# Hybrid decoder step with 64 experts: three of the shared expert's five output tiles moved into the steps 16, 24 and 32 of the expert loop, and the experts' table first filled for four experts

## The reference

```
scores = sigmoid(x @ w_router); top 8 of 64 experts per token (within 4 of 8 groups)
gates  = scores of the chosen / their sum * 2.5
routed = sum over a token's 8 experts of gate * (silu(x @ w1_e) * (x @ w3_e)) @ w2_e
y      = (silu(x @ w1_s) * (x @ w3_s)) @ w2_s  +  routed          # shared expert + routed experts
out    = LayerNorm(ALPHA * x + y)
```

## Time and profile before

| what | value |
|---|---|
| median of three runs | 1242.86 us (1241.7 to 1245.32) |
| the profiled execution: its time | 1241.34 us |
| its span in the trace | 1239.5 us |
| busy PE, DVE, ACT, POOL | 1145.6, 411.7, 257.2, 175.6 us |
| chain that ended last: PE, DMA, DVE | 68%, 15%, 14% of the span |
| HBM read and written | 300.15 and 29.36 MB |

### The profile page before, as it was taken

One profiled execution on the slowest core, in us unless ns is written; L12 is line 12 of the kernel. 1 busy time (PEld: TensorE's weight loads), 2 busy tenths in 40 slices (PEclk: granted clock), 3 DMA queues, 4 the chain that ended last, 5 costly groups with the idle time before them and its releaser, 6 DMA issues.

```text
span 1239.5 us, 21052 instructions
## 1 busy us (share of the span) xinstructions
PE 1145.6 (92%) x8302; PEld 763.2 (62%) x8302; DVE 411.7 (33%) x1016; ACT 257.2 (21%) x564; POOL 175.6 (14%) x208
## 2 busy tenths in 40 slices
PE   7999997999987999889999899998999989989965
PEld 6888645877865688567656565555555556555411
DVE  0359997122067325711221111111211212111124
ACT  1101324022051315011222222221212212212200
POOL 3120040000000000202122122122221222211100
PEclk9999998999999999899999999999999999999977
DMA  9530304034048352619999999999999999999496
GB/s 330 226 136 1 153 12 170 1 135 153 1 141 322 132 216 91 241 51 337 358 378 375 369 376 379 368 376 358 370 370 359 373 378 358 376 359 363 182 357 268
DMA packets 66313, 319.16 MB, mean 257 GB/s; under 512 B 10473, under 2 KB 16833, under 8 KB 39629
## 3 DMA queue, kind: packets, MB, share of 16 engines
q1 hardware_dynamic: 51269, 278.60, 59.5%
q0 software_dynamic: 13568, 35.48, 8.4%
q10 hardware_dynamic: 1424, 4.35, 0.9%
HBM read 300.15 MB, written 29.36 MB: 266 GB/s over the span
## 4 chain that ended last, share of the span: by engine, by line
PE 68%; DMA 15%; DVE 14%; SPq 1%; issue 1%; ACT 1%; DVEq 0%; POOLq 0%
PE psum L744 62%; DMA arena<-in_w_e_dram 10%; DVE act_mem L1698 7%; PE psum L759 6%; DMA arena<-y_rows 3%; DVE mk_mem L1857 2%; DMA arena<-in_w_in_dram 1%; SPq L539 0%; DVE act_mem L1795 0%; DVE act_mem L1712 0%; DVE rstd L1786 0%; DVE act_mem L1793 0%; DVE act_mem L1763 0%; SPq L494 0%; SPq L493 0%
## 5 line engine op out<-in xcount | busy, mean ns | idle before, releaser
L744 PE MATMUL psum<-arena,act_mem 128*32 128x128 f32 (+6 forms) x4800 | 517.0, 365 | 20.8 <-DMA arena<-in_w_e_dram 16.5
L744 PEld LDWEIGHTS psum<-arena,act_mem 128*32 128x32 f32 (+5 forms) x4800 | 266.3, 125 | 210.7 <-issue 118.6
L744 PE MATMUL psum<-act_mem,arena 128*128 128x260 f32 (+1 forms) x1728 | 352.7, 366 | 9.2 <-DMA arena<-in_w_o_dram 3.8
L744 PEld LDWEIGHTS psum<-act_mem,arena 128*128 128x128 f32 x1728 | 306.2, 192 | 53.0 <-DMA arena<-in_w_o_dram 4.7
L759 PE MATMUL psum<-ident,act_mem 96*128 96x96 f32 (+8 forms) x484 | 77.7, 291 | 19.1 <-POOL ident L557 6.8
L667 POOL DMA_INDIRECT y_rows<-act_mem,idx_y x40 | 45.2, 1130 | 323.1 <-DVE idx_x L2074 173.0
L2086 DVE TENSOR_SCALAR act_mem<-psum,act_mem 96x512 f32<-96x512 f32 (+1 forms) x40 | 29.9, 748 | 156.0 <-PE psum L744 156.0
L1698 DVE SCALAR_TENSOR_TENSOR act_mem<-act_mem,wcb 128x511 f32<-128x511 f32 (+29 forms) x120 | 77.7, 725 | 0.0
L759 PEld LDWEIGHTS psum<-ident,act_mem 96*128 96x128 f32 (+8 forms) x484 | 57.5, 175 | 32.3 <-issue 8.0
L2083 DVE TENSOR_TENSOR act_mem<-act_mem,psum 128x192 f32<-128x192 f32 x35 | 12.4, 354 | 191.9 <-ACT act_mem L1554 191.9
L744 PEld LDWEIGHTS psum<-act_mem 128*96 128x96 bf16 (+4 forms) x371 | 28.6, 126 | 57.4 <-issue 51.4
(11 more groups left out here) (262 smaller groups left out, 698.0 us busy)
## 6 DMA issues: line engine op xcount, KB each, us to landing
arena<-in_w_e_dram SPq DMA_DIRECT2D x192, 1024.0 KB
arena<-y_rows SPq DMA_DIRECT2D x8, 2048.0 KB, 23.7
arena<-in_w_in_dram SPq DMA_DIRECT2D x16, 512.0 KB, 18.7
arena<-in_cache_mem_k_dram SPq DMA_DIRECT2D x8, 1024.0 KB, 8.5
arena<-in_cache_mem_v_dram SPq DMA_DIRECT2D x8, 1024.0 KB, 11.4
arena<-in_w_v_dram SPq DMA_DIRECT2D x1, 4096.0 KB, 24.3
arena<-in_w_k_dram SPq DMA_DIRECT2D x1, 4096.0 KB, 13.8
arena<-in_w_out_dram SPq DMA_DIRECT2D x1, 4096.0 KB, 13.8
```

The lines of the kernel that those rows point to most:

```text
L744: return pe.matmul(out, lhsT, rhs, start=first, stop=last)
```

## The change

- `LATE_SO` assigns the tiles 2, 3 and 4 of the shared expert to the steps 16, 24 and 32. In such a step PE runs `shared_out(t)` between `t_step(e-1)` and `c_step(e)`, after waits for the bank of the step before and for a second copy of the weights, `w2s_late` (the place of the first is overwritten in the loop). DVE runs `shared_sum(t)` ahead of its `c_step(e)`; `y_step(e-1)` waits for it.
- Tile 1 is computed between `a_step(1)` and `a_step(2)` as before; tile 0 still comes first. `PAIR` gives them other banks, and the waits that guard the banks move along: `c_step(0)` for tile 0, `y_step(0)` for tile 1, `b_step(0)` for `count`.
- DVE fills the table first for the four experts sorted first (`FIRST`), makes `place` in one operation instead of two (the slot numbers now start at 1), and goes on to the one-hot matrices. `count` and `over` follow after the second one-hot matrix; the table's other 60 experts after `shared_sum(0)`, and `s_table` with them. PE no longer waits for `s_table`.
- SP loads `w2s_late` where it loaded the rows of the last LayerNorm; these are now loaded behind the last expert.
- On PE and DVE the steps 1 to 32 are written out (`UNROLLED`), not 1 to 8.

```diff
+EARLY_SO = 2
+LATE_SO = {t: 2 * NB + NB * (t - EARLY_SO) for t in range(EARLY_SO, TT)}
+PAIR = {f"so{t}": 2 if t == 0 else 0 for t in range(TT)}
+UNROLLED = max(LATE_SO.values()) // NB
+FIRST = 4
...
@@ SP
             wait_out(sp, "count")
-            sp.dma_start(ln3g, ...)
-            sp.dma_start(ln3b, ...)
+            sp.dma_start(w2s_late, I["w2_s"][0].rearrange("(k p) n -> p k n", p=P)).then_inc(s_w2late, 16)
             with sp.Fori(0, E // 4 - 1) as i:
...
+            wait_full(sp, f"so{TT - 1}")
+            sp.dma_start(ln3g, ...)
+            sp.dma_start(ln3b, ...)
...
@@ PE, y_step
+                if isinstance(e, int) and e == 0:
+                    wait_out(pe, "so1")
+                for t, turn_no in LATE_SO.items():
+                    if isinstance(e, int) and e == turn_no - 1:
+                        wait_out(pe, f"so{t}")
...
@@ PE, before the loop
-            shared_out(0)
-            pe.wait_ge(s_table, 1)
-            wait_out(pe, "count")
-            wait_out(pe, "x24")
+            wait_out(pe, "order")
+            shared_out(0, w2s)
...
+            wait_out(pe, "x24")
             a_step(0, 0)
             a_step(1, 1)
-            shared_out(1)
+            wait_out(pe, "rank")
+            shared_out(1, w2s)
             a_step(2, 2)
-            shared_out(2)
             a_step(3, 3)
-            shared_out(3)
-            shared_out(4)
-            wait_out(pe, "so4")
+            wait_out(pe, "count")
             b_step(0, 0, 16)
+            wait_out(pe, "so0")
             c_step(0, 0, 48)
...
@@ PE, step
+                for t, turn_no in LATE_SO.items():
+                    if isinstance(e, int) and e == turn_no:
+                        pe.wait_ge(m_ya, e - 1)
+                        pe.wait_ge(m_yv, len(HEAVY) * i + heavies(k - 2))
+                        pe.wait_ge(s_w2late, 16)
+                        shared_out(t, w2s_late)
                 c_step(e, k % NB, 48 * (2 * i + (k // 4 + 1)))
...
@@ DVE
+            def shares(at):
+                sh, tab = share_p[:, :, at], table[:, :, at]
+                link(dve.tensor_copy(tab[:, :, :, 3], sh))
+                link(dve.tensor_tensor(sh, sh, tab[:, :, :, 3], ALU.subtract))
+                link(dve.tensor_copy(tab[:, :, :, 4], sh))
+                link(dve.tensor_tensor(tab[:, :, :, 5], sh, tab[:, :, :, 4], ALU.subtract))
+            def turns(last, at):
+                for t in range(TT):
+                    n = chain(dve.tensor_tensor_scan(left[:, t, 0:last], wsum[:, 0:last], sel_p[:, t, 0:last], ...))
+                dve.wait_ge(s_v, n)
+                link(dve.tensor_scalar(table[:, :, at, 2], left[:, :, at], 1.0, None, ALU.subtract))
+            shares(slice(0, FIRST))
+            turns(FIRST, slice(0, FIRST))
...
             oh_step(1, 1)
+            wait_full(dve, "count")
...
             shared_sum(0)
-            shared_sum(1)
+            shares(slice(FIRST, E))
+            turns(E, slice(FIRST, E))
+            dve.sem_inc(s_table, 1)
             i_step(2, 2, None)
```

More of the change, by code:

```diff
@@ L78 @@
 TOK = P // TOPK
-PAIR = {f"so{t}": (t + 2) % 3 for t in range(TT)}
+EARLY_SO = 2
[3 more added lines that the diff above has]
+FIRST = 4
 A0, A1, A2, A3, A4 = 0, 4160, 8320, 12480, 16640
@@ L285, in decoder_step @@
         w2s = act_mem[:, 9280:9280 + 2048].rearrange("p (k n) -> p k n", k=2)
+        w2s_late = kv_mem[:, 0:2048].rearrange("p (k n) -> p k n", k=2)
         s_full = sem("s_full")
@@ L1286, in _ @@
             LAST = E // NB - 1
-            for k in range(1, NB + 1):
-                step(k, k, 0)
-            with pe.Fori(1, LAST) as i:
+            for i in range(UNROLLED):
+                for k in range(1, NB + 1):
+                    step(NB * i + k, k, i)
+            with pe.Fori(UNROLLED, LAST) as i:
                 for k in range(1, NB + 1):
@@ L2019, in _ @@
             dve.sem_inc(s_order, 1)
-            link(dve.tensor_copy(table[:, :, :, 3], share_p))
-            link(dve.tensor_tensor(share_p, share_p, table[:, :, :, 3], ALU.subtract))
-            link(dve.tensor_copy(table[:, :, :, 4], share_p))
-            link(dve.tensor_tensor(table[:, :, :, 5], share_p, table[:, :, :, 4], ALU.subtract))
-            for t in range(TT):
-                n = chain(dve.tensor_tensor_scan(left[:, t, :], wsum, sel_p[:, t, :], 0.0, ALU.mult, ALU.add))
-            dve.wait_ge(s_v, n)
@@ L2028, in _ @@
-            link(dve.tensor_scalar(table[:, :, :, 2], left, 1.0, None, ALU.subtract))
-            wait_full(dve, "rank")
-            link(dve.scalar_tensor_tensor(place[:, :, 0:E], bank("rank")[:, 0:TT * E].rearrange("p (t e) -> p t e", t=TT),
-                                          1.0, sel_p, ALU.add, ALU.mult))
-            dve.tensor_scalar(place[:, :, 0:E], place[:, :, 0:E], 1.0, None, ALU.subtract).then_inc(s_emV, 1)
-            wait_full(dve, "count")
-            link(dve.tensor_tensor(mk_mem[:, 520:584], bank("count")[:, 0:E], bump, ALU.add))
@@ new lines, in turns @@
+            def turns(last, at):
+                for t in range(TT):
+                    n = chain(dve.tensor_tensor_scan(left[:, t, 0:last], wsum[:, 0:last], sel_p[:, t, 0:last], 0.0,
+                                                     ALU.mult, ALU.add))
+                dve.wait_ge(s_v, n)
+                link(dve.tensor_scalar(table[:, :, at, 2], left[:, :, at], 1.0, None, ALU.subtract))
+            shares(slice(0, FIRST))
+            turns(FIRST, slice(0, FIRST))
+            wait_full(dve, "rank")
@@ L2039, in _ @@
+            dve.scalar_tensor_tensor(place[:, :, 0:E], bank("rank")[:, 0:TT * E].rearrange("p (t e) -> p t e", t=TT),
+                                     1.0, sel_p, ALU.add, ALU.mult).then_inc(s_emV, 1)
             wait_out(dve, "rank")
-            dve.sem_inc(s_table, 1)
             def shared_sum(t):
@@ L2121, in _ @@
             oh_step(1, 1)
+            wait_full(dve, "count")
+            link(dve.tensor_tensor(counts, bank("count")[:, 0:E], bump, ALU.add))
+            dve.tensor_reduce(cmax, counts, AX.X, ALU.max).then_inc(s_emV, 1)
+            wait_out(dve, "count")
+            dve.tensor_copy(over[:, :], cmax).then_inc(s_over, 1)
             i_step(0, 0, None)
@@ L2126, in _ @@
             shared_sum(0)
-            shared_sum(1)
+            shares(slice(FIRST, E))
+            turns(E, slice(FIRST, E))
+            dve.sem_inc(s_table, 1)
             i_step(2, 2, None)
             oh_step(4, 4)
-            shared_sum(2)
             i_step(3, 3, None)
             oh_step(5, 5)
-            shared_sum(3)
-            shared_sum(4)
+            shared_sum(1)
             c_step(0, 0)
             def step(e, k, i, sc, si):
+                for t, turn_no in LATE_SO.items():
+                    if isinstance(e, int) and e == turn_no:
+                        shared_sum(t)
                 c_step(e, k % NB)
@@ L2145, in _ @@
             LAST = E // NB - 1
-            for k in range(1, NB + 1):
-                step(k, k, 0, None if k <= 2 else 16 * ((k - 1) // 2), None if k < 5 else 16 * ((k - 5) // 2 + 1))
-            with dve.Fori(1, LAST) as i:
+            for i in range(UNROLLED):
+                for k in range(1, NB + 1):
+                    e = NB * i + k
+                    step(e, k, i, None if e <= 2 else 16 * ((e - 1) // 2), None if e < 5 else 16 * ((e - 5) // 2 + 1))
+            with dve.Fori(UNROLLED, LAST) as i:
                 for k in range(1, NB + 1):
```

25 lines of the change are left out of this document (9 added, 16 removed).

## The result

The changed kernel took 1247.51 us (median; 1237.28 to 1253.95 in 20 runs), the kernel before 1242.17 in as many runs beside it: a ratio of 1.0033, 95% interval 1.0019 to 1.0048. It is slower by a third of a per cent; forecast were 1229.0 us (1223 to 1237) and a gain. The profiled execution spans 1247.4 us, against 1239.5 before; its time, 1249.18 us, is 1.7 above the median.

A forecast was written before the change was run, and what follows sets the result against it. Expert loads set the pace from 600 us on, their stream starting a fixed time after the first `c_step`. Gain 14.7 - 1.7 (clock) - 0.7 (written-out steps) = 12.3 us against 1241.34: 1229.0 us, range 1223 to 1237.

The forecast's parts named there:

- Written-out steps: 24 more steps fetched as instructions on PE: 0.25 MB at 370 GB/s, a cost of 0.7 us.
- instruction fetch makes it slower: Rival: 16 fetches in written-out steps stop PE, 1.6 us each, 25.6 us less 12.3 gained: 1254.6 us; chance 0.04.
- The front: Up to the first expert's `b_step(0)` and `c_step(0)`: 14.7 us earlier, less 1.7 for the slow clock.
- the table: DVE's shortened table ahead of the first one-hot matrix: 2.0 us, at 0.25 per small operation and 0.75 for five scans.
- The gather: Gather 0 ahead of `b_step(0)`: issued at 513.0, landing 7.2 us later, with bounds of 3.7 and 11.3 us.
- PE's clock: After 4.3 us of PE idling before `b_step(0)`, the clock halves: 1.7 us charged to `b_step(0)` and `c_step(0)`, at most 3.
- Tiles 2 to 4: Shared-expert tiles in steps 16, 24 and 32: hidden where PE waits for weights, 0 us; uncovered, 3 x 4.2 = 12.6.
- What DVE and POOL now do later: The other 60 experts' table and gathers 2 and 3, after the front: costs nothing; uncovered, 6 us at `b_step(2)`.
- Loads: `w2s_late` replaces LayerNorm rows of as many bytes, now loaded behind expert 63: 0 us, at most 1.
- waits of a microsecond and more without a releaser in the steps 9 to 32: Sign in PE's waits of the changed profile that would show the forecast wrong.
- The DMA share did not fall in the rounds with a tile: Sign in the loop: a fall of the DMA share in rounds with a tile would show the forecast wrong.
- PE did not wait at `b_step(2)`: Sign at the third expert's transposes: a PE wait there would show the forecast wrong.

The follow-up runs named there:

- e9: The kernel before with four rounds written out instead of one, its loop moved by 110 idle TensorE increments placed in waits: 1248.07 us, 1.0037 of before.
- e12: The kernel before with four rounds written out instead of one, its loop moved by 90 idle TensorE increments placed in waits: 1246.48 us, 1.0031 of before.
- e5: The changed kernel with its loop moved by 110 idle TensorE increments placed where PE waits anyway: 1240.12 us, 0.9974 of the kernel before.
- e8: The kernel before with four rounds written out on TensorE and VectorE instead of one, nothing else changed: 1257.6 us, 1.0114 of before.
- e6: The changed kernel with all 64 steps written out and the load of expert 2 held until gather 0 landed: 1232.4 us, 0.9922 of the kernel before.
- e10: e6 with the three tiles at steps 12, 20 and 28 in place of 16, 24 and 32: 1232.39 us, 0.9916 of the kernel before.
- e4: e1 with the loads of experts 2 and 3 issued only when gather 0 has landed: 1240.06 us, 0.9976 of the kernel before.
- e2: The kernel before with 57 idle increments at TensorE's start, moving its loop to the changed kernel's place in a block: 1269.81 us, 1.0218 of before.
- e1: The changed kernel with 110 idle increments at the start of TensorE's stream, moving its loop: 1248.99 us, 1.0053 of the kernel before.
- e11: The changed kernel with gather 0 ahead of experts 2 and 3's loads, tiles at steps 4, 6, 8, one round written out: 1238.95 us, 0.9958 of before.

## Why the prediction was wrong

**The step that failed is "Written-out steps", at 0.7 us.** Measured are 15.1 us from expert 4 to expert 63. I priced a fetch by its bytes, 24 steps at 370 GB/s, and took from one stretch that its latency is hidden. Two things were wrong in this.

First, the 24 written-out steps by themselves cost 4 to 5 us (e9, e12; e5 loses 5.0 between experts 4 and 63). The stretch from 640 to 720 showed no fetch on the chain although the loop was fetched there for the first time: it is no written-out code, as step 9, the first of the loop, began its product at 628. PE waited there for weights too (2.75 us at step 16) and 0.93 us without a releaser at 686; four rounds in a row, with tiles in three of the waits for weights, had less to hide in. That the fetches are what costs the 4 to 5 us is argued, not shown.

Second, and twice as dear: the change moved the loop. Nothing in the prediction asked whether the loop, which cost no fetch before, would still stay in the buffer at its new place. It did not: 10 us (15.1 less 5.0, after against e5), 9.5 by time between e8 and e9, 7.4 between the changed kernel and e5. (The first figure compares two single executions; the profiled one of e5 lies 2.7 us below its median and that of the changed kernel 1.7 above.) Each of the changed kernel's jumps back stalls 4.1 or 5.4 us, and PE comes out of it with the clock down. The rows that could have raised the question were in the profile: no instruction fetch from 720 to 1100 in a program that is 37 packets long.

The Trainium skill, "Runtime: NRT & Kernel Launch" (Instruction fetch mechanics), says that TensorE's buffer holds 2048 instructions and is refilled in blocks of 256, that its refill runs ahead in order, and that a taken branch to a block outside the current window of two blocks stalls for a fetch. The trace agrees with the stall (4.11 and 5.36 us), and the seven or eight blocks fit the size. It differs on the window: the kernel before jumps back over more than six blocks without a fetch. The page also says that the cost of crossing a block is mostly hidden; e9's 18 more packets go with 4 to 5 us.

The rival "instruction fetch makes it slower" named the mechanism with a chance of 0.04. Its price was 1.6 us for each of 16 fetches, 25.6 us, and 0.8 us was where it would have turned the gain. The runs show 18 more packets and 4 to 5 us for the straight steps, some 0.25 us each, and 18 more for the two jumps back. The rival counted the straight steps and not the loop: with those alone (e5) the kernel is faster than before, so its direction came out by luck, through the loop, which it did not name.

**The front was mis-sized: 13.0 us forecast, 8.5 measured** (7.1 at the load of expert 4, plus the 1.4 by which this execution's prefix was late). The chain of waits after, which answers to the earlier trace rows:

```profile
508.40 1.37 DVE act_mem L2035
...
514.03 0.15 DVE idx_x L2076
...
515.06 9.94 DMA act_mem<-x_rows,idx_x
...
525.14 1.73 PE psum L768 x8
...
527.93 9.86 PE psum L753 x64
```

Order and places are as forecast; three terms are off, by 0.7, 2.7 and 0.9 us, nearly all of the 4.5. The cast of 128x20 took 1.37 us, not 0.25, and the table 2.84 (508.40 to 511.24) instead of 2.0, which puts the gather 0.7 behind its forecast. The kernel before could have told: its first cast took 1.87 us and the next one, of the same shape, 0.70, some 1.2 less, as in the changed kernel (1.37 and 0.21). In both, the first cast overlaps POOL's clearing of two buffers, and in the changed one it ends with it. That the clearing is the cause, no run tells. The rows before (two) and after:

```profile
506.50 1.85 POOL L645 MEMSET act_mem<- 128x1024 f32 x2
...
509.57 0.70 DVE L2023 CAST act_mem<-kv_mem 128x320 bf16<-128x320 f32 x1
```

```profile
507.86 1.85 POOL L654 MEMSET act_mem<- 128x1024 f32 x2
```

The gather landed 9.9 us after its issue, not 7.2; the bounds of 3.7 and 11.3 held it, and I chose the nearer row where the fuller queue was the better likeness. With the loads held back it took 4.4 (e6). The prediction's estimate from the Trainium skill, "DMA: Bandwidth & Descriptors" (Anatomy of one DMA), was 3.1 us for a lone gather and 4.1 at half rate; 4.4 is near it, 9.9 beside the loads is not.

PE's clock took 2.6 us, not 1.7: the first transposes 1.73 instead of 1.16, the first product 9.86 instead of this of the kernel before:

```profile
537.09 7.79 PE L744 MATMUL psum<-act_mem,arena 128*128 128x112 f32 x64 [1.01 <-ACT act_mem L1544]
```

The granted clock there, in the changed kernel:

```profile
518.00:525.00 7.00, 0.00 (x0) 0.00 (x0) 6.58 (x18) 0.00 (x0) 1.84 (x2) 0.81 1.03 356
525.00:527.00 2.00, 1.73 (x8) 1.42 (x8) 0.93 (x1) 0.09 (x1) 1.69 (x2) 0.50 1.03 338
527.00:530.00 3.00, 2.07 (x10) 2.10 (x11) 0.00 (x0) 0.83 (x1) 0.28 (x1) 0.50 1.01 381
```

**What held.** *Tiles 2 to 4* cost nothing, as forecast: from the load of expert 18 to that of 19, from 26 to 27 and from 34 to 35, the changed kernel's issue times, taken against before as in the table, move by 0.3 us at most. (3.67 and 0.75 add up to 4.4, not to the 4.2 of the prediction; nothing hung on it.) The tile of step 16 and the product behind it:

```profile
689.26 3.67 PE L753 MATMUL psum<-kv_mem,act_mem 128*128 128x512 f32 x8 [0.61 <-ACT act_mem L1580]
693.30 5.83 PE L753 MATMUL psum<-arena,act_mem 128*64 128x256 f32 x96 [0.37 <-issue]
```

The product takes 5.83 us instead of 7.42: the slow clock is gone with the wait. But the reason was narrower than the truth; e10 shows that the tile need not stand at the wait. *What DVE and POOL now do later* cost nothing: PE waited 8.4 us for gathers in all, 7.6 of it for the first. *Loads*: no run sets the load of the late weights apart; it is among what e4 and e6 hold back behind the gather. The sum as these two executions have it: 8.5 for the front, less 1.4 for this prefix, less 5 for the written-out steps, less 10 for the jumps back, 7.9 slower; the spans differ by 1247.4 - 1239.5 = 7.9. (The 5 and the 10 are a split of one measured 15.1, so the sum does not test them; e8 and e9 do.)

The prediction's own list of signs would not have found this. It named "waits of a microsecond and more without a releaser in the steps 9 to 32"; the longest there is 0.90 us, at 661. The DMA share did not fall in the rounds with a tile, and PE did not wait at `b_step(2)`. The longer waits, 1.40 us at 906 and the two stalls with 1.81 behind the second, all lie in the loop, in steps it did not think of.

## What to carry to other kernels

When an edit lengthens an engine's program ahead of a loop, ask where the loop comes to stand in the blocks in which instructions are fetched, before asking what the edit's instructions cost; compare the instruction queue's packets in the loop before and after, and test the place with idle instructions put into waits. Price straight code by a run with more of it written out, not by the bytes fetched. And when a wait is about to hide new work, count waits a round: each can be spent once, on work that stands at it or ahead of it.

## What the hardware showed that I had not expected

- 57 idle instructions on TensorE made a kernel 27 us slower (e2, 1.0218), through five stalls of 5.5 us at the loop's jumps back.
- An increment of a semaphore on TensorE takes some 0.15 us (the estimate under e1), so that padding ahead of a loop must stand in waits (e1 against e5: 8.9 us for the same 110 instructions).
- A gather of 112 rows of 4 KB lands 4.4 us after its issue with a quiet queue and 9.9 us beside loads that were issued ahead of it; holding two loads of 3 MB and one of 1 MB back cost nothing later (e6, where PE waits for no expert weights).
- The clock fell after short idle times too. In e6, where PE idled 2.0 us, the first transposes ran at a granted clock of 0.50, that is 1.2 GHz. In e11, after 1.9 us, they still ran at 1.00, and the clock fell only in the product behind them, which took 9.29 us against 9.47. The stretches of e6 (first) and e11:

```profile
519.40:522.00 2.60, 1.73 (x8) 1.41 (x8) 2.53 (x7) 0.80 (x1) 0.00 (x0) 0.50 0.44 112
```

```profile
519.40:522.00 2.60, 1.41 (x11) 1.30 (x11) 2.53 (x7) 0.92 (x1) 0.00 (x0) 1.00 0.48 110
522.00:525.00 3.00, 3.00 (x17) 3.00 (x16) 2.72 (x10) 0.00 (x0) 1.84 (x2) 0.53 0.90 369
```
